# Expert weights of a mixture-of-experts stage in halves of 2 MB with rows of 4 KB, in a ring of eight, in place of quarters of 1 MB with rows of 2 KB in a ring of sixteen

## What is computed

```
def ec_ffn(h, w_router, b_router, w_gate, w_up, w_down):
    n_tok = h.shape[1]
    cap = CAP_FACTOR * n_tok // N_EXP
    def route_set(hs):
        aff = jax.nn.softmax((hs @ w_router + b_router).astype(jnp.float32), axis=-1)
        gate, idx = lax.top_k(aff.T, cap)
        xe = hs[idx]
        hid = jax.nn.silu(jnp.einsum('ecd,edf->ecf', xe, w_gate)) * jnp.einsum('ecd,edf->ecf', xe, w_up)
        ye = jnp.einsum('ecf,efd->ecd', hid, w_down) * gate[..., None].astype(hid.dtype)
        return jnp.zeros(hs.shape, ye.dtype).at[idx.reshape(-1)].add(ye.reshape(-1, hs.shape[-1]))
    return jax.vmap(route_set)(h)
```

## Time and profile before

| | us |
|---|---|
| median of 3 runs | 4144.21 |
| lowest and highest | 4141.35, 4151.69 |
| profiled execution, its own time | 4156.34 |
| its span, first to last instruction | 4153.8 |
| PE busy | 3661.3 (88%) |
| DVE busy | 2216.6 (53%) |
| ACT busy | 1061.6 (26%) |
| loads of expert weights | 384 of 1 MB, 402.7 MB of the 542.3 MB on SP's queue |

### The profile page before, as it was taken

How to read it: one execution, slowest core, us unless ns; L and a number is a source line. 1 busy time by engine, 2 the same in 40 slices (tenths; PEclk the granted TensorE clock), 3 DMA queues, 4 the chain that set the end, 5 groups by cost and what they waited for, 6 DMA issues and landing times. The chain is left out here.

```text
span 4153.8 us, 65794 instructions
## 1 busy us (share of the span) xinstructions
PE 3661.3 (88%) x27258; PEld 2037.1 (49%) x27258; DVE 2216.6 (53%) x3672; ACT 1061.6 (26%) x2344; POOL 484.0 (12%) x675
## 2 busy tenths in 40 slices
PE   6899999777897599999997899998697865999998
PEld 4555675576733233333333755674586532333333
DVE  3454324687755444444443445335778666565654
ACT  3342110544311111111112443112544211211121
POOL 1100000221201011111111200000232110010110
PEclk9999999688998799999998899998698987999999
DMA  6300120200175667777774100111100335999996
GB/s 239 113 1 11 56 77 0 78 13 19 45 275 202 229 224 263 263 262 263 263 255 137 36 21 11 58 69 42 47 10 13 119 133 213 333 328 316 336 318 213
DMA packets 291446, 613.12 MB, mean 148 GB/s; under 512 B 37544, under 2 KB 45992, under 8 KB 284496
## 3 DMA queue, kind: packets, MB, share of 16 engines
q1 hardware_dynamic: 270608, 542.32, 36.7%
q0 software_dynamic: 20544, 66.60, 6.2%
HBM read 561.07 MB, written 47.79 MB: 147 GB/s over the span
## 5 line engine op out<-in xcount | busy, mean ns | idle before, releaser
L3010 PE MATMUL ps<-moe_w,e_hT 128*128 128x512 f32 x1024 | 450.0, 598 | 16.7 <-DMA moe_w<-in_w_down_dram 8.7
L3127 DVE TENSOR_TENSOR moe_w<-moe_w 128x2048 f32<-128x2048 f32 x128 | 287.3, 2286 | 204.7 <-PE ps L2945 160.0
L2915 PE MATMUL ps<-moe_w,e_xs 128*64 128x512 f32 x1536 | 348.6, 596 | 0.0
L2915 PE MATMUL ps<-moe_w,e_xT 128*64 128x512 f32 x1536 | 344.2, 597 | 0.0
L3010 PEld LDWEIGHTS ps<-moe_w,e_hT 128*128 128x128 f32 x1024 | 193.0, 191 | 254.5 <-issue 253.5
L3133 DVE TENSOR_TENSOR e_cb<-e_part,ps 128x512 f32<-128x512 f32 x128 | 87.7, 685 | 346.0 <-ACT e_part L3047 259.3
L2915 PEld LDWEIGHTS ps<-moe_w,e_xT 128*64 128x64 f32 x1536 | 111.0, 138 | 221.4 <-issue 221.3
L2915 PEld LDWEIGHTS ps<-moe_w,e_xs 128*64 128x64 f32 x1536 | 105.0, 137 | 193.2 <-issue 192.6
L3047 ACT COPY e_part<-ps 128x512 f32<-128x512 f32 x96 | 56.2, 585 | 507.6 <-PE ps L2915 507.6
L1207 PE MATMUL ps<-M 96*128 96x512 f32 (+1 forms) x400 | 182.8, 543 | 3.2 <-PEq L913 2.1
L1097 PE MATMUL ps<-yT,hT 128*128 128x272 f32 (+1 forms) x608 | 146.7, 396 | 9.6 <-PEq L262 9.2
(11 more groups left out here) (422 smaller groups left out, 7060.5 us busy)
## 6 DMA issues: line engine op xcount, KB each, us to landing
moe_w<-in_w_gate_dram SPq DMA_DIRECT2D x128, 1024.0 KB, 13.7
moe_w<-in_w_up_dram SPq DMA_DIRECT2D x128, 1024.0 KB, 14.1
moe_w<-in_w_down_dram SPq DMA_DIRECT2D x128, 1024.0 KB, 13.1
o_mod_w<-in_w_ada_dram SPq DMA_DIRECT2D x24, 1024.0 KB, 7.6
m_mod_w<-in_w_ada_dram SPq DMA_DIRECT2D x16, 1024.0 KB, 5.7
yT<-in_w_in_dram SPq DMA_DIRECT2D x6, 2048.0 KB, 7.8
r_z<-z_rows SPq DMA_DIRECT2D x20, 512.0 KB, 3.3
z_rows<-p_zo POOLq DMA_DIRECT2D x36, 256.0 KB, 2.3
```

The costliest lines, as they stand in the source:

```text
L2915: ins = nc.tensor.matmul(ps[HF * q:HF * q + HF, b, :], x[:, k], weights[q][:, k], start=(first and k == 0), stop=(k == 3), skip_group_chec ...
L3010: ins = nc.tensor.matmul(ps[:, YB + c, :], hT2[:, 4 * half + k], quarter(name, e)[:, k], start=(half == 0 and k == 0), stop=(half == 1 and ...
L3127: nc.vector.tensor_tensor(to, a, b, ALU.subtract).then_inc(*td.up())
```

## The change

The parts are halves: `g1` is rows 0 to 511 of the gate matrix with all its columns (the former `g11` and `g12`), and `d1` holds `d0` and `d1` of before. A part is 2 MB, with rows of 4 KB in memory and in SBUF, and the ring has eight places, so it is as large as before. The products still read quarters, as views with a step of 1024 between rows of 512. SP's waits follow: the place of a first half is free after P7, that of a second half after P3.

```
-MOE_RW = 16
-MOE_ORDER = [("g11", 0), ("u11", 0), ("g21", 0), ("u21", 0), ("g12", 0), ("u12", 0), ("g22", 0), ("u22", 0),
-             ("d0", -1), ("d1", -1), ("d2", -1), ("d3", -1)]
+MOE_RW = 8
+MOE_ORDER = [("g1", 0), ("u1", 0), ("g2", 0), ("u2", 0), ("d1", -1), ("d2", -1)]
...
-    half, c = divmod(int(name[1]), 2) if name[0] == "d" else (int(name[1]) - 1, int(name[2]) - 1)
+    half = int(name[1]) - 1
...
-    sp.dma_start(g.moe_w[:, j % MOE_RW], src[:, 4 * half:4 * half + 4, 512 * c:512 * c + 512]).then_inc(*g.sg(f"w_slot{j % MOE_RW}").up(16))
+    sp.dma_start(g.moe_w[:, j % MOE_RW], src[:, 4 * half:4 * half + 4]).then_inc(*g.sg(f"w_slot{j % MOE_RW}").up(16))
...
+        def half_of(name):
+            if name[0] == "d":
+                return f"d{int(name[1]) // 2 + 1}", int(name[1]) % 2
+            return name[:2], int(name[2]) - 1
         def quarter(name, e):
-            return w[:, PART_AT[name, e] % RW]
+            h, c = half_of(name)
+            return w[:, PART_AT[h, e] % RW, :, 512 * c:512 * c + 512]
         def quarter_in(eng, name, e):
-            j = PART_AT[name, e]
+            j = PART_AT[half_of(name)[0], e]
...
-                            sp.wait_ge(*dm.at(4 * eo + int(name[1]) + 1))
+                            sp.wait_ge(*dm.at(4 * eo + 2 * int(name[1])))
                     else:
-                        sp.wait_ge(*product_at(eo, {"11": P5, "12": P7, "21": P4, "22": P3}[name[1:]]))
+                        sp.wait_ge(*product_at(eo, {"1": P7, "2": P3}[name[1]]))
...
-            with nc.sbuf_tensor(f"moe_w{l}", [P, MOE_RW, 4, 512], F32) as g.moe_w:
+            with nc.sbuf_tensor(f"moe_w{l}", [P, MOE_RW, 4, 1024], F32) as g.moe_w:
```

## The result

| | us |
|---|---|
| changed kernel, median of 4 runs | 4259.82 (4252.93 to 4269.98) |
| kernel before beside it, median of 4 runs | 4147.95 (4141.35 to 4154.21) |
| ratio | 1.0265, 95% interval 1.0240 to 1.0289 |
| profiled execution of the changed kernel | 4269.98, the slowest of its four |
| its span | 4267.5, before 4153.8: +113.7 |

The change costs 2.65%. The prediction said 4231 in a range of 4195 to 4285 and "slower" with 0.95: right in sign, cause and range, 29 us too low.

The account below looks back on a forecast made before the run. PE was taken as the bound in the experts of both layers. Stalls before P2 75, down projection 3, old waits -12 and clock 21 sum to +87 us on the 4144.2 median: 4231, range 4195 to 4285.

Parts of the forecast that it names:

- The release decides: Ring of expert weights: g2 and u2 get places free only after P7, so P2 waits 28 times, +75 us.
- the period of an expert: Sign named in advance: one expert would take 55.4 us in layer 0 and 43.6 to 44 in layer 1.
- The stall of 2.66: PE before P2: 4 MB land in 12.61 us against 10.14 available, so 2.66 us idle, 28 times.
- So the bounds are 0 and 1.7 us a stall, and I take 0: Extra delay of the new load pair from other traffic such as POOL's gather and scatter: taken as 0 per stall.
- Rate: Full load queue with rows of 4 KB: 412 GB/s, between 387 at 2 KB and 426 at 8 KB.
- The rival that has rows of 4 KB cut in two: Load queue splits 4 KB rows, rate unchanged: stall 3.32 us, +109 us, 4253; no chance of its own given.
- The clock: PE's clock falls after one stall in four, slowing work behind it: 7 x 3.05 = +21 us, ends 0 and 85.
- at almost every stall: Rival: PE's clock falls at almost every stall before P2, +151 us, 4295; chance 0.10.
- Down projection and old waits: Down projection: d1 slightly late, +3 us; earlier waits for w_down and their clock fall go, -12 us.
- Weights sooner: Rival: longer rows and fewer transfers at 438 GB/s, stall 2.06 us before P2, +46 us, 4190; chance 0.07.
- Other traffic: Rival: new load pair loses 1.7 us to other traffic, stalls 4.36 us, +138 us, 4282; chance 0.09.
- Faster: Rival: 4 MB land within 10.14 us, P2 never waits, the -12 us remains, 4132; chance 0.03.

Follow-up runs that it names:

- e2: Changed kernel with the same loads in the same order put in other ring places, so g2 and u2 take places free long before; 4136.31 us, ratio 0.9968.
- e1: Changed kernel with each half loaded by two 1 MB DMAs with rows of 2 KB, places and order kept; 4292.46 us, ratio 1.0351.
- e7: Changed kernel with the place of a first half given back after P4 instead of P7, one product later; 4386.90 us, ratio 1.0576.
- e5: Changed kernel run once more, unedited, to see how its executions differ; 4267.14 us, ratio 1.0298.
- e3: Kernel with e2's places, each half loaded by two 1 MB DMAs with rows of 2 KB; 4137.12 us, ratio 0.9980.

## Why the prediction was right, and what was mis-sized

**The release decides: right.** Same loads, other places: all 28 waits vanish (e2). Same places, other loads: they stay (e1). Release moved by a product: they grow by about a product (e7). One sign that I had named was missed: the period of an expert is 57.7 us in layer 0 and 45.1 in layer 1 in the mean, not 55.4 and 43.6 to 44, because waits and clock cost more than forecast.

**The stall of 2.66: right for an undisturbed pair, low in the mean.** The pair at 3647.41 landed after 12.71 us (12.61 forecast), and P2 started 2.79 late against its old spacing. Fifteen of the 28 waits are like it: 2.46 to 2.76, mean 2.64, or 2.81 with the 0.17. The other thirteen are longer, mean 3.25 in six and 4.03 in seven. "So the bounds are 0 and 1.7 us a stall, and I take 0" was the step that failed: traffic does meet the new pair. It isn't POOL's gather, which I had looked at. The queues in the 12.8 us before the landing of the pair that took 14.6 us (packets, MB, share of 16 engines), then in the 12.9 us around the one that took 12.71:

```profile
q1 hardware_dynamic: 1286, 5.14, 101.2%
q8 instruction: 1, 0.02, 0.5%
```

```profile
q1 hardware_dynamic: 1147, 4.57, 88.3%
```

All seven waits of 3.72 to 4.46 us have such a packet of the instruction queue q8 (16 KB each by the page's count: 219 packets, 3.59 MB) between the issue of the pair and P2; all six of 3.01 to 3.41 have one of q14 (8 KB each) instead; none of the fifteen short ones has either. A packet of q8 keeps one DMA engine for about 1.0 us (0.5% of 16 engines over 12.8 us). In e5 the same split gives 2.72 (16 waits), 3.23 (7) and 4.0 (5), in e1 3.13 (16), 3.63 (6) and 4.47 (6). The split is not quite clean there: each has one packet of q8 within 0.1 us of the pair's issue, before any data of it moves, and the waits behind these two, 2.82 and 3.63, are counted with the short ones.

Run e7, which shifted every pair by 3.43 us, moved some pairs off their packet. The same expert in the changed kernel and in e7:

```profile
1720.91 5.35 PE L2921 MATMUL ps<-moe_w,e_xT 128*64 128x512 f32 x16 [4.04 <-DMA moe_w<-in_w_up_dram]
...
1737.82 5.90 PE L2921 MATMUL ps<-moe_w,e_xT 128*64 128x512 f32 x16 [6.12 <-DMA moe_w<-in_w_up_dram]
```

It and two more waits whose packet of q8 no longer falls among the pair's data grew by 2.0 to 2.2 us, while the fifteen that have no packet in either trace grew by 3.4 to 4.0. Packets of q8 in the first 0.4 us behind the issue go with no more (6.12) or with up to 1.7 us more (7.92) than e7's undisturbed 6.19. A load is spread over 16 DMA engines and is complete with the last of them, so that one engine which also serves a long packet delays all of it: that is my reading. The extra wait follows the packets, but no run changed the packets alone, so the mechanism is argued, not shown. The Trainium skill ("Runtime: NRT & Kernel Launch", section on instruction fetch mechanics) says that engines fetch instructions in blocks of 16 KB over DMA queues of their own, and calls this mostly hidden. The block size agrees with q8's packets; the waits behind such packets, 1.4 us longer, were not hidden from a PE that waits for a load. In numbers: 6 x 0.61 + 7 x 1.39 = 13 us of the 17 by which the idle time was forecast too low; the other 4 are 28 x 0.15 of the undisturbed pair.

**Rate: right.** 409 GB/s against 412 interpolated from the earlier trace rows. The Trainium skill's fixed 3 cycles a packet ("DMA: Bandwidth & Descriptors", section on why small descriptors are slow) would have given 396 and stalls 0.3 us longer than the undisturbed ones are. Rows of 2 KB instead of 4 lengthen the undisturbed wait from 2.64 to 3.13 (e1), by 0.49 where the forecast had 0.66. The rival that has rows of 4 KB cut in two falls: its rate was 387.

**The clock: more often, and cheaper.** "I take one in four: 7 x 3.05" became 19 slow P2 and 35 us. Both factors were wrong, and in opposite directions: 19 at 3.05 would have been 58 us, so that the term is only 14 us off is in part luck. Twelve of the 14 in layer 0 fell, 7 of the 14 in layer 1; by waits, 7 of the 15 short ones, 5 of the 6 middle ones, 7 of the 7 long ones. So between 2.5 and 2.8 us of idle time about half of the P2 came back slow, which of them I can't say from these traces, and my two rows at 2.34 and 2.78 that showed none were too few to read "one in four" from. And one fall costs mostly 5.35 - 3.65 = 1.70 us here, in three cases 2.7 to 3.0; the 3.05 was that of a fall behind 3.33 us. The rival "at almost every stall" was nearer in count, but at its 3.05 a fall it came to 85 us, more than twice what was lost.

**Down projection and old waits: right.** -7 against -9, and e2, without any late w_down, is 11 us below the kernel before where these waits had been put at 12.

**At nothing: right.** SP's issues (192 in place of 384), DVE's sums, the stages outside.

**Rivals.** Weights sooner (stall 2.06) fell with the rate: 409, not 438. Other traffic (4.36 at every stall) happened at a quarter of them, from another source. "Faster" had the right mechanism, that early enough weights give the 12 us: e2 is that case, reached through the places and not through speed.

## What to carry to other kernels

In a ring of buffers the place of a part decides when its load may start; the order of issue decides only its turn. Before parts are made larger, write down for each what lay in its place, when that is last read, and how long before its own first use that is: here 10.1 us for a load that needs 12.7. The places can be chosen apart from the order, so that each part follows one whose last use is long past; that version (e2, 4136 us) has the large transfers and is 0.3% under the kernel before, level with the same places and small transfers (e3, 4137).

## What the runs showed of the hardware

- A load of 4 MB in two transfers into an idle queue took 12.7 us where no packet of an instruction queue fell into it, and about 0.6 (q14) and 1.4 us (q8) longer where one did, by the waits behind it. Behind three pairs that e7 shifted off their packet of q8 most of this extra was gone.
- Full-queue rates from memory: 387 GB/s with rows of 2 KB, 409 with 4 KB, 426 with 8 KB.
- PE behind 2.5 to 2.8 us of idle time came back at full clock in 8 of 15 cases and lower in 7 (in e5, 8 of 16); a lower one cost mostly 1.7 us, and the work behind P2 was at full speed again (13.97 us for the projection). Why layer 0 falls more often (12 of 14) I have not settled; its long waits are part of it, but of the short ones too 4 of 6 fell there against 3 of 9 in layer 1.
